# A hybrid decoder step on one Trainium2 core: the delta-rule preparation in another order, with block updates by transposition

## The reference, cut to what matters

```python
qkv = jax.nn.silu(conv)                       # conv of 4 taps over x @ w_in
q = _l2norm(q) * (DK ** -0.5)
k = _l2norm(k)
b = jnp.cumsum(ac, axis=-1)                   # within a chunk
diff = b[..., :, None] - b[..., None, :]
L = einsum(kc, kc) * exp(where(strict, diff, -inf)) * bc[..., :, None]
rhs = concatenate([vc * bc[..., None], kc * (bc * exp(b))[..., None]], axis=-1)
sol = triangular_solve(L + eye(c), rhs, lower=True, unit_diagonal=True)
P = einsum(qc, kc) * exp(where(causal, diff, -inf))
def step(S, xs):                              # over the chunks, in order
    W = u_ - wk_ @ S
    o = qd_ @ S + p_ @ W
    S = cd_ * S + kd_.T @ W
```

## Time and profile before

| | |
|---|---|
| median of 3 executions | 2808.83 us (2807.74 to 2809.3) |
| profiled execution | 2808.29 us |
| span of its trace, first to last instruction | 2806.6 us |
| PE busy | 95% of the span |
| DVE busy | 46% |
| ACT busy | 29% |
| mean granted TensorE clock | 0.974 of full speed |

### The profile page before, as it was taken

The page is one execution under the profiler, slowest core; times in us unless marked ns, Lnnn a source line. Parts: engine busy times, 40 slices in busy tenths (PEclk is TensorE's granted clock), DMA queues, the critical chain, the costliest instruction groups (busy, mean ns, idle before and its releaser), DMA issues.

```text
span 2806.6 us, 49074 instructions
## 1 busy us (share of the span) xinstructions
PE 2652.6 (95%) x20705; PEld 2538.2 (90%) x20705; DVE 1304.8 (46%) x1653; ACT 821.3 (29%) x1045; POOL 305.5 (11%) x307
## 2 busy tenths in 40 slices
PE   7999999999999999999999999898889889999997
PEld 6999998888888899999999999788788778999997
DVE  4444234646463644433344433565546645544323
ACT  3222222323232432222222222333423332322222
POOL 1000001202020200000100001003410343100000
PEclk9999999999999999999999999999999999999999
DMA  4332233515152433323433323220011200333231
GB/s 121 91 90 81 80 103 109 189 64 191 62 186 67 145 88 90 90 75 89 117 90 90 85 81 89 92 78 16 31 67 61 63 31 20 91 90 90 72 93 62
DMA packets 340962, 246.81 MB, mean 88 GB/s; under 512 B 9540, under 2 KB 322044, under 8 KB 340832
## 3 DMA queue, kind: packets, MB, share of 16 engines
q1 hardware_dynamic: 326480, 197.32, 23.9%
q0 software_dynamic: 14352, 47.58, 4.6%
HBM read 218.81 MB, written 26.05 MB: 87 GB/s over the span
## 4 chain that ended last, share of the span: by engine, by line
PE 83%; DVE 9%; ACT 4%; issue 4%; POOL 1%; DMA 0%; SPq 0%; DVEq 0%; POOLq 0%; ACTq 0%
PE ps L720 56%; PE ps L904 11%; PE ps L1092 6%; ACT wh L1242 1%; PE ps L802 1%; DVE cv L1832 1%; DVE wl L1532 1%; PE ps L757 1%; PE ps L1036 1%; PE ps L811 0%; PE ps L1043 0%; PE ps L823 0%; PE ps L1010 0%; PE ps L1048 0%; DVE xl L1538 0%
## 5 line engine op out<-in xcount | busy, mean ns | idle before, releaser
L1532 DVE TENSOR_TENSOR wl<-raw,wh 128x2048 fp32r<-128x2048 f32 (+1 forms) x204 | 427.5, 2095 | 344.0 <-ACT wh L1242 344.0
L720 PE MATMUL ps<-xh,wh 128*128 128x260 f32 x2816 | 569.6, 283 | 4.9 <-DVE gate L2059 4.4
L720 PE MATMUL ps<-xh,wl 128*128 128x260 f32 x2816 | 568.8, 284 | 0.0
L720 PE MATMUL ps<-xl,wh 128*128 128x260 f32 x2816 | 568.0, 283 | 0.0
L1242 ACT ACTIVATE wh<-raw 128x2048 fp32r<-128x2048 f32 (+1 forms) x204 | 354.5, 1738 | 348.4 <-PE ps L720 212.2
L720 PEld LDWEIGHTS ps<-xh,wh 128*128 128x128 f32 x2816 | 436.1, 189 | 6.5 <-issue 5.2
L720 PEld LDWEIGHTS ps<-xh,wl 128*128 128x128 f32 x2816 | 435.6, 189 | 0.0
L720 PEld LDWEIGHTS ps<-xl,wh 128*128 128x128 f32 x2816 | 434.4, 189 | 0.0
L720 PE MATMUL ps<-hh,wh 128*128 128x260 f32 x1408 | 287.7, 286 | 13.5 <-DVE hl L2064 13.5
L720 PE MATMUL ps<-hl,wh 128*128 128x260 f32 x1408 | 285.4, 284 | 0.0
L720 PE MATMUL ps<-hh,wl 128*128 128x260 f32 x1408 | 285.4, 284 | 0.0
(11 more groups left out here) (352 smaller groups left out, 3034.6 us busy)
## 6 DMA issues: line engine op xcount, KB each, us to landing
raw<-in_ffn_gu_dram SPq DMA_DIRECT2D x176, 512.0 KB, 4.9
raw<-in_ffn_down_dram SPq DMA_DIRECT2D x64, 384.0 KB, 3.5
raw<-in_ret_w_in_dram SPq DMA_DIRECT2D x48, 512.0 KB, 4.5
raw<-in_ffn_down_dram SPq DMA_DIRECT2D x64, 320.0 KB, 3.9
s_ring<-in_state_ret_dram POOLq DMA_DIRECT2D x32, 512.0 KB, 6.8
out_dram<-s_ring POOLq DMA_DIRECT2D x32, 512.0 KB, 3.1
raw<-in_gdn_w_in_dram SPq DMA_DIRECT2D x32, 512.0 KB, 4.6
raw<-in_ret_w_out_dram SPq DMA_DIRECT2D x16, 512.0 KB, 4.4
```

Of the source, the lines that this page charges most:

```text
L720: m_ = nc.tensor.matmul(ps[:, 2 * q + h, 0:HALF], w_, v[:, kt0 + t, h * HALF:(h + 1) * HALF], start=b_, stop=e_)
L1532: nc.vector.tensor_tensor(wl[:, s, 0:cols], raw[:, s, 0:cols], wh[:, s, 0:cols].bitcast(F32), ALU.subtract).then_inc(w_low, 1)
```

## The change

The matrices `t`, `a` are made as before. The changes are:

1. In each level `b` (a product of `t` and `m`, 8 rows) is not computed. PE transposes the updated `mt` (4 rows) at the start of the next level, and ACT copies the even blocks of it into `m`. ACT's filling of `t` with zeros (`z`) and DVE's subtraction of `b` go. `a` is formed on the odd blocks alone, 64 columns a head where it was 128.
2. `br` and `wr` are made from a broadcast column and a constant matrix (`rows_of`, 4 matmuls of 128 columns where it was one of 512), so that DVE no longer makes `aut` and `dg`.
3. The inverse root is formed at the start of DVE's unit 10, and the spreads stand after and in the middle of units 10 to 13, where they stood after units 12 to 14. Gate unit 14 moves into the first pair's preparation, unit 15 into the second's.
4. The preparation goes chunk by chunk: the second chunk of a pair begins when the first has its scores and mask, and level 1 of the first chunk stands within the second's preparation.
5. Of chunk 2, `kt`, `vt`, `kk`, `br`, `dd`, `n2`, `eb` are done among the states of chunks 0 and 1. On POOL the stores of the sample states come ahead of `s2`.
6. The splits of weight slots 8 and 9 (the output projection), the root of the first norms and the gate's SiLU move to levels 2 to 4.

```diff
+SPREAD_AFTER = {(10, 1): [0], (11, 0): [1], (11, 1): [2], (12, 0): [3], (12, 1): [4, 5], (13, 0): [6], (13, 1): [7]}
+SPREAD_BANK = (4, 4, 4, 4, 4, 6, 4, 6)
+SPREAD_BEFORE = {1: 0, 2: 1, 3: 2, 4: 3, 6: 4, 7: 5}
...
                     if n == 0:
                         v("rl")
...
+                    if n in SPREAD_BEFORE:
+                        v(f"dq{SPREAD_BEFORE[n]}")
...
-                for n in range(15):
+                for n in range(14):
...
+                def rows_of(bank, column, right, name):
+
+                    for h in range(GG):
+                        m_ = nc.tensor.matmul(ps[:, bank, h * P:(h + 1) * P], column(h).broadcast_to([P, P]), right, start=True, stop=True)
+                    did(m_, name)
...
+                    def middle(l, c, bb, ch):
+                        pe.wait_ge(gdn_p, Q(f"l{l}.{c}", g))
+                        if l == 1:
+                            act_(f"mt.{c}")
+                        else:
+                            v(f"a{l - 1}.{c}")
+                            for h in range(GG):
+                                m_ = nc.tensor.transpose(ps[:, bb + 2, h * P:(h + 1) * P], ch["mt"][:, h, :], ident[:])
+                            did(m_, f"b{l - 1}.{c}")
+                            act_(f"t{l - 1}.{c}")
+                        four(bb + 3, ch["lb" if l % 2 else "la"], ch["mt"], f"t{l}.{c}")
...
-                            four(bb, ch["m"], ch["t1"], f"a{l}.{c}")
-                            if l < LV:
-                                four(bb + 2, ch["t1"], ch["m"], f"b{l}.{c}")
...
+                    unit(14 + p)
+                    scores_and_mask(*both[0])
+                    if p == 0:
+                        pe.wait_ge(acc_free, ph.unit0 + GDN_UNITS * g + 15)
+                        decay_rows(1, 0)
...
+                    middle(1, *both[0])
+                    change(1, *both[0])
...
+                    scores_and_mask(*both[1])
...
+                        if c == 0:
+                            key_scores(2, 7, gk, "kk")
+                            decay_rows(2, 4)
+                        if c == 1:
+                            turned(2, 6, gv, "vt")
...
                 for n in range(12):
+                    if n == 10:
+                        act_("rt")
+                        did(nc.vector.reciprocal(roots[:], roots[:]), "ri")
...
+                    if n == 10:
+                        normed(0)
+                    if n == 11:
+                        normed(2)
...
+                normed(3)
+                split_next(6)
+                normed(4)
+                normed(5)
+                gate_unit(0)
+                normed(6)
+                normed(7)
+                gate_unit(1)
```

More of the change, by code:

```diff
@@ L1050, in sample_step, with decay_rows, turned, key_scores @@
                             did(m_, f"os{b}")
+                def decay_rows(c, bb):
+                    rows_of(bb, lambda h: small[:, 5, c, h0 + h:h0 + h + 1], ut, f"br.{c}")
+                def turned(c, bank, src, name):
+                    for h in range(GG):
+                        m_ = nc.tensor.transpose(ps[:, bank, h * P:(h + 1) * P], src[:, h, c * P:(c + 1) * P], ident[:])
+                    did(m_, f"{name}.{c}")
+                def key_scores(c, bank, other, name):
+                    at_ = slice(c * P, (c + 1) * P)
+                    for h in range(GG):
+                        m_ = nc.tensor.matmul(ps[:, bank, h * P:(h + 1) * P], gk[:, h, at_], other[:, h, at_], start=True, stop=True)
+                    did(m_, f"{name}.{c}")
@@ L1052, in gdn_body @@
                 for p in range(2):
                     both = [(2 * p + x_, 4 - 4 * x_, chain[x_]) for x_ in range(2)]
[L1054 to L1077, removed]
@@ L1078, in gdn_body, with scores_and_mask @@
-                    for c, bb, ch in both:
-                        at_ = slice(c * P, (c + 1) * P)
+                    def scores_and_mask(c, bb, ch):
                         act_(f"kd.{c}")
-                        for h in range(GG):
-                            m_ = nc.tensor.matmul(ps[:, bb + 1, h * P:(h + 1) * P], gk[:, h, at_], gq[:, h, at_], start=True, stop=True)
-                        did(m_, f"qk.{c}")
+                        key_scores(c, bb + 1, gq, "qk")
                         act_(f"vb.{c}")
@@ new lines, in change @@
+                    def change(l, c, bb, ch):
+                        act_(f"t{l}.{c}")
+                        if l == 1:
+                            v("ssA" if c == 3 else f"dd.{c}")
+                            act_(f"eb.{c}")
+                        else:
+                            act_(f"b{l - 1}.{c}")
+                        for h in range(GG):
+                            m_ = nc.tensor.matmul(blocks(ps[:, bb, h * P:(h + 1) * P], l, 1), ch["m"][:, h, :], blocks(ch["t1"][:, h, :], l, 1),
+                                                  start=True, stop=True)
+                        did(m_, f"a{l}.{c}")
@@ new lines, in gdn_body @@
+                    middle(1, *both[0])
+                    change(1, *both[0])
+                    if p:
+                        v("dd.3")
+                        act_("eb.3")
+                        for h in range(GG):
+                            act_(f"sqA{h}")
+                            did(nc.tensor.matmul(ps[0:GH, 0, part["A"]], gather(h), gsq[:, h, part["A"]], start=h == 0, stop=h == GG - 1), f"nnA{h}")
+                    scores_and_mask(*both[1])
+                    for l in range(1, LV + 1):
+                        for c, bb, ch in both[1:] if l == 1 else both:
+                            middle(l, c, bb, ch)
@@ new lines, in gdn_body @@
+                    key_rows(*both[0])
+                    decays_and_rows(*both[0])
+                    if p:
+                        act.wait_ge(gdn_a, A("oc.1", g))
+                        for h in range(GG):
+                            square(h, "A")
+                    mask_turned(*both[0])
+                    decayed(*both[1])
+                    key_rows(*both[1])
+                    middle(1, *both[0])
+                    decays_and_rows(*both[1])
+                    mask_turned(*both[1])
@@ new lines, in gdn_body @@
+                            if l > 1 or c % 2:
+                                middle(l, c, bb, ch)
+                        if p and l == 2:
+                            v("ssA")
+                            root("A", roots_o[:, part["A"]])
+                        if l == 3:
+                            split_next(7 + p)
+                        if p and l == 4:
+                            act.wait_ge(acc_free, ph.unit0 + GDN_UNITS * g + 16)
+                            nc.scalar.activation(gz[:], gz[:], ACT.Silu).then_inc(gdn_a, A.did("sz"))
```

259 lines of the change are left out of this document (131 added, 128 removed).

## The result

The changed kernel takes 2789.03 us (median of 4 executions, 2780.46 to 2790.3) where the kernel before takes 2809.07: ratio 0.9928, 95% interval 0.9914 to 0.9942. It is 20 us faster, and 46 us were forecast; the range began at 2747 and ended at 2781. The profiled execution took 2788.71 us, 1.6 more than its span.

A forecast was written before the change was run, and what follows sets the result against it. PE was taken as the bound, busy 2652.6 of 2806.6 us. Terms -12 - 31.1 - 15.5 + 10 gave -48.6, a second way -43.3; -46 was taken, for a median of 2763 us, range 2747 to 2781.

The forecast's parts named there:

- Levels, -3.0 us a pair: Levels 2 to 6: dropping b saves 7.1 us, transpositions add 4.4; net -3.0 a pair, -12 for four.
- the clock falls in the levels: Rival: transpositions lower PE's clock in levels 2 to 6, up to +116 us, 2879 at full price; chance 0.03.
- A, -31.1: First pair's preparation, unit 10's end to level 2: 51.9 us at full clock, so -16.8 and -14.3.
- wait for the first spread: In A, behind unit 10: PE waits 4.0 us for rl, costing another 1.7 us (up to 3.4) in clock.
- Chunk 1's chain, 2.5 a group: In A: PE busy about 2.2 of 6.6 us during chunk 1's score-to-mask chain, losing 2.5 us of clock (1.7 to 3.4).
- B, -15.5: First state product to level 2 of the second pair: 34.0 us at full clock, so -9.2 and -6.3.
- Clock after, +10: Clock loss left in A and B after the change: 5 us a group, 10 in all, with ends 0 and 20.
- sum of -48.6: Whole kernel: levels -12, A -31.1, B -15.5, clock +10; a second way gave -43.3, and -46 was taken.
- B never falls below the share that kept 1.00: B stays busy enough for full clock, but for one place: 0.8 us lost (0 to 3.4).
- the clock stays as it was: Rival: the new 4 us wait and chunk 1's chain cost clock like the old waits, 23.2 for 10: 2776; chance 0.13.
- The levels wait: Rival: copies come 0.5 us too late in each of 20 levels, +10 us: 2773; chance 0.18.
- nothing comes of it: Rival: waits only change places and each transposition costs as much as a product; within 0.2%; chance 0.02.

The follow-up runs named there:

- wide samples: The changed kernel with the sample-step rows r and os multiplying their one column broadcast to 128 equal columns: 2758.56 us alone, 0.9813 of the kernel before.
- later spreads: The changed kernel with the first spread in the middle of unit 11 instead of behind unit 10, the others half a unit later: 2777.98 us alone, 0.9897.

## Why the prediction was wrong in size and right in direction

- **Levels, -3.0 us a pair.** The work was right: 34.98 x 0.83 = 29.0 us in the changed kernel, and 29.32 and 30.19 measured at full clock with wide samples, where 29.1 and 30.0 follow from the forecast. "PE is busy in all of them" was right too. What failed is the step from there to the clock: that the full clock of the levels before would stay because PE stays busy. The sum had no term for it. It cost (1 - 0.83) x 34.98 and its like, 23.3 us in four pairs, and this is most of the miss.
- **The rival "the clock falls in the levels"** had 0.03 and is what happened, at a fifth of its full price of 116. Its reason, that transpositions don't count, is not what the runs show: 7 us of them alone kept the clock where 7 us of one-column rows lost it, and levels full of them stood at 1.00 once the sample rows were wide. My argument against it failed as well. I held 80% busy against a stretch that was busy for 3.34 of 4 us; but rows of one column are busy time like any other in the profile, and they were the ones that mattered. `os` was among the prices at 0.81 us, and nothing was asked of its width.
- **By the Trainium skill**, "TensorE: Matmul & The Clock Gate", Part 4 (PE-mode transpose), a transposition doesn't count as busy the way a matmul does. The trace disagrees for the f32 transpositions here: 7.15 us of them, clock 1.00. Whether one counts in full beside narrow rows stays open.
- **The cause, as shown.** The change took the wide `b` away and halved `a` around one-column rows that had been harmless. Any one of three edits heals all eight places behind levels 3 and 5 (wide `os`, wide `a`, products in place of the transpositions), so the mixture decided, not one kind of row; the weakest rows in it are those of one column. `r`, 32 rows of one column in two blocks, goes with the fall at the start of level 2: with `r` at one column it stands in 31 pairs of 32 in eight versions of the changed kernel, whatever `a`, `os` and the transpositions are, and only widening `r` to 128 took it away in all four. The kernel before has the same 32 rows and no fall in its levels; there they stood between wide products. Which part of that difference counts, the packing of `r` or the missing `b`, no run separates: none put `r` back apart.
- **A, -31.1.** The walk gave 51.9 us at full clock, 52.0 and 51.7 came out, partly by luck: PE idles 8.4 and 8.0 us where 11.6 of waits were walked, and its busy time at full clock is some 43.6 us where 40.3 were. A part of this is only a way of counting (a group of eight rows stands as 1.06 us busy in the profile and was priced at the 0.89 to the next start); the rest are waits walked too long and work priced too low, and they cancelled. The wait for the first spread was 3.7 and 3.4 for 4.0. Its price in clock, 1.7 (up to 3.4), measured 3.4 and 1.7. Chunk 1's chain, 2.5 a group, measured 4.1 and 0.6 up to the end of A, in a fall that `r` carries on into the levels.
- **B, -15.5.** 34.0 walked, 34.43 measured where the clock was full; 3.0 us of it idle where 4.5 were walked.
- **Clock after, +10.** The mis-sized term. One minus clock times length is 10.5 us in A and 6.0 in B, 16.5 for 10; with the levels 39.8. These 29.8 us more are, to within rounding, the whole distance of 29.0 between the sum of -48.6 and the -19.6 that came. "B never falls below the share that kept 1.00" failed because its end holds `r`: with a wide `r` it stands at 1.00. Outside the levels the clock cost more than forecast and less than in the rival "the clock stays as it was" (23.2).
- **"The levels wait"** and **"nothing comes of it"** did not happen: PE is busy 34.98 of 34.98 us in a level stretch, and four transpositions took 0.44.

The version with wide samples and later spreads takes 2748.41 us, 61 less than the kernel before and 41 less than the changed one.

Besides what is called open above, two things are. Why the fall at the start of level 2 was absent in one pair of four with both `a` and `b` as wide products: it was one profiled execution, and where a fall comes differs from one to the next. And what a half-width row counts for beside others: alone it kept the clock, in the mixture its widening healed it.

## What to carry to other kernels

A busy TensorE is not yet one at full clock: before a change takes wide matmuls away, look at what is left around the narrow ones, and read the granted clock level by level. Four f32 matmuls cost nearly the same with 1 column (0.81 to 0.87 us), 64 (0.84 to 0.92) and 128 (0.89 to 0.98, from start to start), so narrowing an operand saves little and can cost the clock; broadcasting a single column to 128 cost next to nothing (levels of 29.3 us, where 29.0 at full clock follow for one column) and was worth 30 us here. A wait in front of dense work costs its length and, here, nearly as much again in clock (5.7 us of waits, 11 us of time). And a sum that comes out right is not yet a walk that was right: hold its parts against the trace too.

## What the runs showed of the hardware that was not expected

- 7.15 us of f32 transpositions (64 rows) left the clock at 1.00; 8 groups of products with 32 columns or with one, of about the same time, took it to 0.50 for part of the levels.
- The same narrow rows were harmless beside wide ones: the levels of the kernel before hold `os` with one column at clock 1.00, and widening all its sample rows gave 5.7 us where the changed kernel gained 30.
- Executions of one kernel lie up to 11 us apart: the changed one 2780.46 to 2790.3, the one with products in place of the transpositions 2790.6 to 2801.61. The places where the clock falls and their lengths differ from one trace to the next. In the second preparation A, up to the start of level 2, a fall takes some 2 us in the changed kernel and 12 with the later spreads, though the rows there are the same; outside the mixer, 20 to 40 us from the start, the clock is 1.00 in the kernel before and 0.71 in the changed one.
